# Streaming encoder step: attention scores from stacked high and low parts, two maps a step, layers written out

## What is computed

```python
for l in range(DEPTH):                       # DEPTH = 2
    h = rms_norm(x, norm_mix[l]);  q, k, v = split(h @ w_in[l])      # q and k normalised per head
    A: 6 heads of 64, window of 128, T5 bias, a learned sink:   p = exp(s-m) / (sum + exp(sink-m))
    B: 4 heads, two maps of 32 each, T5 bias:  p = softmax(s1) - lam * softmax(s2)
    C: 6 heads of 64, causal, s += cum_q - cum_k (forget gates)
    x = x + concat(A, B, C) @ w_out[l]
    x = x + (silu(h2 @ w_gate) * (h2 @ w_up)) @ w_down               # h2 = rms_norm(x, norm_ffn[l])
```

## Time and profile before

| | |
|---|---|
| median of 3 runs | 3513.45 us (3509.74 to 3520.22) |
| the profiled execution's span | 3514.1 us |
| TensorE busy | 3223.0 us (92%) |
| VectorE / ScalarE busy | 1718.7 us (49%) / 1076.7 us (31%) |
| mean granted TensorE clock | 0.967 of 2.4 GHz |
| DMA | 275 MB, 27.5% of 16 engines |
| first layer: project, attend, mix, feed | about 137 to 408, to 824, to 942, to 1797 us |
| second layer, same stages | about 1840 to 2120, to 2537, to 2655, to 3514 us |

### The profile page before, as it was taken

How to read it: one execution, slowest core, us unless ns; L and a number is a source line. 1 busy time by engine, 2 the same in 40 slices (tenths; PEclk the granted TensorE clock), 3 DMA queues, 4 the chain that set the end, 5 groups by cost and what they waited for, 6 DMA issues and landing times. The chain is left out here.

```text
span 3514.1 us, 50348 instructions
## 1 busy us (share of the span) xinstructions
PE 3223.0 (92%) x18146; PEld 2884.4 (82%) x18146; DVE 1718.7 (49%) x4094; ACT 1076.7 (31%) x2321; POOL 54.3 (2%) x32
## 2 busy tenths in 40 slices
PE   0699899998899999999969997999898999999999
PEld 0589777786789999999958896777777999999998
DVE  0444378643244544545445445785434454454454
ACT  1332276553221111111123225665423111111111
POOL 0000010000000000000000001010000000000000
PEclk9899999998999999999989998999998999999999
DMA  7244544333021111111024445525132111111111
GB/s 170 79 138 133 161 122 106 88 82 116 18 66 36 41 49 36 53 37 36 24 92 124 132 136 138 131 69 137 35 94 59 44 36 54 36 36 54 36 36 60
DMA packets 368396, 274.96 MB, mean 78 GB/s; under 512 B 128546, under 2 KB 336366, under 8 KB 368186
## 3 DMA queue, kind: packets, MB, share of 16 engines
q1 hardware_dynamic: 368218, 272.70, 27.5%
HBM read 195.84 MB, written 78.62 MB: 78 GB/s over the span
## 5 line engine op out<-in xcount | busy, mean ns | idle before, releaser
L1515 DVE TENSOR_TENSOR x<-x,ffn_down 128x512 f32<-128x512 f32 x792 | 509.4, 683 | 0.0
L1537 DVE TENSOR_TENSOR ffn_xn<-ffn_xn,ffn_up 128x384 f32<-128x384 f32 x132 | 73.1, 554 | 758.1 <-ACT ffn_xn L1482 758.1
L418 PE MATMUL ffn_up<-ffn_h_hi,ffn_hi_g 128*128 128x384 f32 x1056 | 360.3, 341 | 15.2 <-DVE ffn_h_lo L243 10.5
L419 PE MATMUL ffn_up<-ffn_h_lo,ffn_hi_g 128*128 128x384 f32 x1056 | 359.7, 341 | 0.0
L420 PE MATMUL ffn_up<-ffn_h_hi,ffn_lo_g 128*128 128x384 f32 x1056 | 359.4, 340 | 0.0
L418 PE MATMUL ffn_up<-ffn_h_hi,ffn_hi_u 128*128 128x384 f32 x1056 | 355.2, 336 | 3.2 <-DVE ffn_lo_u L243 3.2
L420 PE MATMUL ffn_up<-ffn_h_hi,ffn_lo_u 128*128 128x384 f32 x1056 | 354.8, 336 | 0.0
L419 PE MATMUL ffn_up<-ffn_h_lo,ffn_hi_u 128*128 128x384 f32 x1056 | 354.8, 336 | 0.0
L991 PE MATMUL att_S<-att_kT,att_qT 128*128 128x512 f32 (+3 forms) x864 | 322.9, 490 | 33.1 <-DMA att_qT<-scratch_qkT 25.9
L1482 ACT ACTIVATE ffn_xn<-ffn_up 128x384 f32<-128x384 f32 x132 | 64.9, 491 | 861.1 <-PE ffn_up L420 861.1
L418 PE MATMUL prj_acc<-prj_w_hi,prj_h_hi 128*128 128x384 f32 (+2 forms) x864 | 318.8, 369 | 0.0
(11 more groups left out here) (173 smaller groups left out, 5352.5 us busy)
## 6 DMA issues: line engine op xcount, KB each, us to landing
ffn_raw_g<-in_w_gate SPq DMA_DIRECT2D x44, 512.0 KB, 4.0
ffn_raw_u<-in_w_up SPq DMA_DIRECT2D x44, 512.0 KB, 5.1
ffn_raw_d<-in_w_down SPq DMA_DIRECT2D x44, 512.0 KB, 5.1
scratch_qkv<-prj_nat SPq DMA_DIRECT2D x72, 192.0 KB, 1.9
prj_w_raw<-in_w_in SPq DMA_DIRECT2D x64, 192.0 KB, 2.6
scratch_qkv<-prj_nat SPq DMA_DIRECT2D x36, 256.0 KB, 2.1
att_kT<-scratch_qkT SPq DMA_DIRECT2D x16, 576.0 KB
att_vn<-scratch_qkv SPq DMA_DIRECT2D x16, 576.0 KB, 8.4
```

Of the source, the lines that this page charges most:

```text
L418: pe.matmul(out, l_hi, r_hi, start=first, stop=False)
L419: pe.matmul(out, l_hi, r_lo, start=False, stop=False)
L1515: dve.tensor_tensor(x, x, down[:, (q * ND + n) % 4, :], ALU.add).then_inc(added, 1)
L1537: dve.tensor_tensor(a32[:, b, :], sg[:, b, :], up[:, b, 1, 0:384], ALU.mult).then_inc(gated, 1)
```

## The change

The two layers are written out instead of looped, and semaphores and tiles get the layer's number (`att0_scored`). Beyond that:

1. **project** splits the transposed q and k into high and low parts (`tT_hi` on ScalarE in place of the copy, `tT_lo` a new subtraction on VectorE, `cut_turned`) and stores both (`qk`), where it stored one. Sample rows are also stored whole (`qk_s`). The store of all rows to `scratch_qkv` shrinks to the value columns (`v`). `tT` has two buffers, not four.
2. **attend, scores**: in `qS` the 128 contraction rows hold the high part over the low part of one map's q; `kS` holds the key's high part twice (first matmul) and its low part twice (second). In B, with 32 rows a map, all four products fit one matmul. The data are f32r. Scores against cached keys stay float32.
3. **attend, steps**: a unit in A and C is now two heads (9 units a group), and in B one head with two maps (18) as before. Every unit has two jobs.
4. **attend, softmax**: the reduction forms bias minus score with its minimum, so its result is the exponential's bias and the one-column instructions go. The sink enters as column 0 of s. In C a column of ones behind v gives the row sum.
5. **attend, samples**: in A and C one matmul multiplies both heads; the result goes to `mixTb` without being turned back. A1 and A2 reuse A0's cached keys and values.
6. **memory**: x is given up during `attend`; `mix` reloads it (4 MB and 0.5 MB) behind the loads of g = 3. POOL no longer clears q.

```diff
@@ build
-        with nc.Fori(0, DEPTH) as layer:
+        for layer in range(DEPTH):
             project(nc, t, k, layer)
+            stream.close()
             attend(nc, t, k, layer)
+            stream = ExitStack()
+            k["x"] = stream.enter_context(nc.sbuf_tensor(f"x_{layer}", [P, T, D_MODEL], F32))
             mix(nc, t, k, layer)
             feed(nc, t, k, layer)
...
@@ project, VectorE
+            def cut_turned(u):
...
+                dve.wait_ge(taken_qk, m + 1)
+                split_lo(dve, tT_lo[:, m % 2, 0:n], turn[:, m % 2, 0:n], tT_hi[:, m % 2, 0:n]).then_inc(cut_qk, 1)
...
@@ attend, SP: load_front of A and C
-                for m in range(g.maps):
-                    sp.dma_start(qT[m * g.D:(m + 1) * g.D, b, m, :], t["qkT"][g.q_row(m):g.q_row(m) + g.D, :]).then_inc(sem, 16)
+                        sp.dma_start(qS[:, b, m, :].bitcast(F32), rows(t["qk"], q0, [[half, 2], [TOK, HEAD], [1, TOK]])).then_inc(sem, 16)
+                        if g.new_keys:
+                            for part in range(2):
+                                sp.dma_start(kS[:, b, 2 * m + part, :].bitcast(F32),
+                                             rows(t["qk"], part * half + k0, [[0, 2], [TOK, HEAD], [1, TOK]])).then_inc(sem, 16)
...
@@ attend, TensorE: score
+                    ks = [m] if g.kind == "B" else [2 * m, 2 * m + 1]
...
-                            last = pe.matmul(out[:, c:c + w], q, kT[:, b, k0 + c:k0 + c + w], start=True,
-                                             stop=not (g.kind == "C" and c + w == n))
+                            for x in ks:
+                                last = pe.matmul(out[:, c:c + w], q, kS[:, b, x, k0 + c:k0 + c + w], start=(x == ks[0]), stop=(x == ks[-1] and not masks))
...
@@ attend, VectorE: front
-                    dve.tensor_tensor_reduce(s[:, job % 2, 0:n], S[:, job % 2, 0:n], extra_row, 1.0, -3e38, ALU.add, ALU.max, mx[:, one]).then_inc(biased, 1)
+                    dve.tensor_tensor_reduce(s[:, r, g.sink:g.sink + n], S[:, r, 0:n], extra_row, -1.0, low, ALU.add, ALU.min,
+                                             bias[:, job:job + 1]).then_inc(biased, 1)
...
@@ mix, SP and VectorE
+                if g == 3:
+                    sp.dma_start(k["x"][:, 0:TP, :], t[prompt].rearrange("a (t p) d -> p (a t) d", p=P)).then_inc(x_in, 16)
+                    sp.dma_start(k["x"][:, TP, :], t[sample].rearrange("b s d -> (b s) d")).then_inc(x_in, 16)
...
+            dve.wait_ge(x_in, 32)
```

More of the change, by code:

```diff
@@ L123, in _ @@
                 numbers = sorted(s.num for s in self.sems)
-                assert numbers == list(range(numbers[0], numbers[-1] + 1))
-                pool.sem_clear(range(numbers[0], numbers[-1] + 1))
+                first = 0
+                for n in range(1, len(numbers) + 1):
+                    if n == len(numbers) or numbers[n] != numbers[n - 1] + 1:
+                        pool.sem_clear(range(numbers[first], numbers[n - 1] + 1))
+                        first = n
         self.ctx.close()
@@ L433, in stores @@
         flat = f"({shape})"
+        if name[2] == "v":
+            out.append((t["v"][i * P:(i + 1) * P, V_AT[first]:V_AT[first] + count], src))
         if sample:
@@ L494, in project, with samples_before @@
     order = [sum(bool(NORMED[v[0]]) for v in work[:u]) for u in range(NW)]
+    def samples_before(m):
+        return sum(work[normed_units[x]][1] == TP for x in range(m))
     def splits_at(u):
@@ L849, in attend @@
         for c in range(g.past_chunks):
-            extra.setdefault(g.index * UG + 2 + c, []).append(("past", g, c))
-        for c in range(3):
-            extra.setdefault((g.index + 1) * UG + 7 + c, []).append(("mix", g, c))
-    N_ITER = NU + 11
+            extra.setdefault(begin[g.index] + 2 + c, []).append(("past", g, c))
+        after = begin[g.index + 1] + (7 if g.kind == "B" else 3)
+        for c in range(3 if g.kind == "B" else 2):
+            extra.setdefault(after + c, []).append(("mix", g, c))
+    N_ITER = NU + 6
     order = []
@@ L952, in _ @@
                     load_front(groups[g.index + 2])
-                sp.wait_ge(evacuated, place["mix", g.index, 2] + 1)
+                sp.wait_ge(evacuated, last_mix[g.index])
+                if g.kind != "B":
+                    sp.wait_ge(taken_T, before(begin[g.index + 1], direct))
                 sp.dma_start(t["mixT"][g.tile * P:(g.tile + 1) * P, :], mixTb[:]).then_inc(mix_stored, 16)
@@ L999, in score @@
                                       start=(c == 0), stop=(c == g.nb - 1))
[L1000 removed]
+                        for x in ks:
+                            last = pe.matmul(out[:, g.n_past:g.n_samp], q, kS[:, b, x, SEQ:TOK], start=(x == ks[0]), stop=(x == ks[-1]))
                     last.then_inc(scored, 1)
@@ L1034, in turn_extra @@
                     elif c == 0:
-                        pe.wait_ge(taken_out, (g.index + 1) * UG)
+                        pe.wait_ge(taken_out, before(begin[g.index + 1], lambda *x: not direct(*x)))
                     a, e = chunk_of_mix(c)
@@ L1262, in mix @@
 def mix(nc, t, k, layer):
-    ph = Phase(nc, "mix")
+    ph = Phase(nc, f"mix{layer}")
     BANKS = 8
```

442 lines of the change are left out of this document (258 added, 184 removed).

## The result

The changed kernel takes **4254.8 us** (median of 4 runs, 4253.3 to 4264.9) against 3514.0 for the kernel before: a ratio of **1.212**, 95% interval 1.210 to 1.214. It is 741 us slower. I had forecast 3419 with a range up to 3465, so the prediction was wrong in sign and by 836 us.

A forecast was written before the change was run, and what follows sets the result against it. TensorE was taken to bound project and attend, with VectorE close behind in B and taking over there. Per layer A -12, B -25, C -19, end -2, mix +10.5 make -47.5, twice -95: 3419 us, range 3380 to 3465.

The forecast's parts named there:

- Loads, start of attend: Attend: extra q and k bytes at 340 to 390 GB/s cost A0 +6.5 us, B0's front +1, later groups nothing.
- loads weigh more: Rival, loads of q and k: at 250 GB/s about 13 us a layer more, 3445 us; chance 0.13.
- The slow case: Rival, B: TensorE's clock stays at half level throughout, 3557 us, slower than before; chance 0.02.
- A: Attend's A groups: cheaper scores and no turning back save 3.2, 4.1 and 4.1 us; POOL's dropped clearing of qT saves 8.
- B: Attend's B groups: VectorE becomes the limit, 111 us instead of 139.2, -28, and +3 for B0's cached keys.
- hand-overs: B: pauses between engines add 3 us to the limiting engine's work.
- My signs for B: Profile after, B: 111 to 115 us, VectorE busy over 90%, TensorE near 80%; a clock below 0.9 would be wrong.
- C: Attend's C groups: TensorE stays the limit; -5.6 us a group and -2 for POOL's clearing in C0, -19 a layer.
- The rival of the narrow pieces: Rival, scores of 128 or 256 columns: they cost what float32 costs, 3495 us; chance 0.03.
- Mix: Mix: reloading x delays g = 4's loads, a stall of 8 us and +2.5 for the half-level clock, together +10.5.
- Project: Project: 26 us more VectorE work is hidden, 0; if the cover fails in the first nine units, +4.
- The milder one: Rival, B: TensorE's clock falls for half of its 90 us, +8 to +12 a layer, 3437 us; chance 0.10.

The follow-up runs named there:

- e1: Changed kernel with the first two dimensions of the source pattern exchanged in every load of qS and kS, row number outermost: 3446.1 us.
- e4: e1 with each of B's loads of qS and kS writing every second one of all 128 partitions in place of 64 neighbouring ones: 3422.1 us.
- e5: e4 with mix's load of x put behind the loads of g = 7 in place of g = 3: 3418.2 us.
- e8: The kernel of e4 again, in more rounds and on the same chip as e9: 3427.3 us.
- e9: The kernel of e5 again, in more rounds: 3417.8 us.
- e10: e9 with project's subtraction that forms the low part of q and k run on 1 column in place of 256 to 512: 3415.4 us.

## Why the prediction was wrong, step by step

**Loads, start of attend: the step that failed.** It counted bytes (3.5 MB for A0, 6.1 for B0) and divided them by the rate of the earlier trace rows. But that rate is one of transfers with 32 to 128 rows outermost, and the change replaces these by transfers with a pair outermost. The diff in the section on the change shows it, `[[half, 2], [TOK, HEAD], [1, TOK]]`, and I read past it. What I put down as +6.5 for A0's loads was, in TensorE's waits, 77.7 us in place of 13.1: +65. B0's front, +1, was 78.0. A1's loads, which I took as nothing, cost 57.1, and those of B1 and C, "in the shadow", 66.4 and 131.4. What failed is the rate, and with it the overlap. My rival "loads weigh more" had the right place, but its worst rate was 250 GB/s, four times what the trace of after shows (63), so even the range left the real cause out. The slow case that I did name, a clock that stays down through B, is not what made the kernel slower: with the loads mended the same work takes 3446.1. A rate taken from a trace belongs to the shape of transfer that made it.

With this one term mended (e1), the rest of the sum can be held against what happened. Layer 1, from the ends of groups and stages in e1's trace and in that of before (attend starts with POOL's first clearing, 411.8 us before and 416.1 in e1):

| part | forecast, us | measured in e1, us |
|---|---|---|
| start of attend to A2's end (B0's wait left out) | -13 | 95.4 to 75.5: -20 |
| B with B0's waits | -24 | 139.2 to 135.8: -3 |
| C and the end of attend | -21 | 195.9 to 177.2: -19 |
| mix | +10.5 | 99.5 to 104.0: +4.5 |
| project | 0 | +4 (and +8 in layer 2; see below) |
| loop written out | 0 | 11.7 to 7.3 between the layers: -4, once |
| both layers and the whole | -95 | 3514.1 to 3447.6: -66.5 |

**A: right mechanism, too small.** A2 takes as long as A1 once POOL no longer clears qT, as forecast. The group ends of e1 show both at 19.5 us (forecast: 22):

```profile
452.67 0.95 POOL L1035 MEMSET att_qpast<- 128x1024 f32 x1 [35.54 <-PE att_S L1070]
472.15 0.95 POOL L1035 MEMSET att_qpast<- 128x1024 f32 x1 [18.53 <-PE att_S L1070]
491.62 0.95 POOL L1035 MEMSET att_qpast<- 128x1024 f32 x1 [18.52 <-PE att_S L1070]
```

In A1 TensorE is busy for all of it, 19.50 of 19.50 us; before it was 25.18 of 26. The saving of 6.5 is 5.7 of work and 0.8 of pauses; I had counted 4.1. By the distances between starts the scores fell from 7.9 to 4.4 us (-3.5, where I had -2.7), the rest of the work by 2.2 (where I had 1.4): the samples' matmuls, which I had not counted, are part of it. The remaining clearings of qpast cost nothing that shows.

```profile
453.60:473.10 19.50, 19.50 (x174) 19.45 (x174) 11.79 (x57) 15.18 (x51) 0.97 (x2) 1.00 0.37 123
```

**B: the waits and TensorE's work were too small.** Of the 21 us that e1's B fell short, e4 gives back 8 (B takes 128.0 there) through the packets' length. The rest went where I had 3 us of hand-overs. My signs for B failed too: VectorE was to be busy for over 90% of it and is for 74% in e1 and 78% in e4. TensorE's work is 105.0 us in e1 and not 90, as much as VectorE's. Of the 15 us more, about 9 are an estimate for the half clock (18.6 us of the work ran at it). The other 6 are not split further; part of them is the first score matmul of a map, behind which the next one starts after 0.31 us and not 0.23. A sum of each engine's work over a group assumes that the slower one works without pause, and 569 to 593 us show that the two take turns: 61.6 us in B1 where VectorE's work alone is 54. VectorE's work itself, 100 us in B0 and B1, was less than my 107.5.

**C: right.** TensorE stays the limit (forecast 49.4 us a group; C1 takes 51.7). The prices held. TensorE in e1's C1, where a unit of 1024 keys has two heads:

```profile
709.00 1.17 PE L1061 MATMUL att_S<-att_kS,att_qS 128*128 128x512 f32 x4
710.00 0.23 PE L1063 MATMUL att_S<-att_mask_b,att_ident_b 128*128 128x128 bf16 x1
710.04 1.17 PE L1061 MATMUL att_S<-att_kS,att_qS 128*128 128x512 f32 x4
711.06 0.23 PE L1063 MATMUL att_S<-att_mask_b,att_ident_b 128*128 128x128 bf16 x1
```

Two pieces of 512 columns in two passes take 1.0 us, start to start, where before the same took 1.78. Behind the first matmul of a head the next starts after 0.31, 0.26, 0.20 and 0.14 us for 512, 384, 256 and 128 columns; behind the others after 0.23, 0.17 and 0.12, the three values that I used, and 0.06 for 128. For a piece of 128 columns in two passes that makes 0.20, near my 0.22. The rival of the narrow pieces falls.

**Mix: right mechanism, too large.** The pause before g = 4 is 3 us instead of 8, because x came at 400 GB/s and TensorE reached g = 4 a us later than before; and no fall of the clock followed, for which I had 2.5. (The 8 were themselves a slip: 14 us of x behind 857.76 make 872 and not 870, a pause of 10.)

**Project: a little more than nothing.** It takes 4 us more in layer 1 of e1 and 8 in layer 2, but the 8 is one profile: in the changed kernel, e4, e5, e8 and e9 the second layer has 1.6 to 4.5 more than before, the first 3.3 to 5.5. e10 gives some 1 to 3 us of this to the subtraction; where the rest and the shorter step between the layers (-4) come from, no run tells.

**The clock.** In e1's B it is 0.84 and 0.94 on average, 0.89 over both groups and 0.85 in layer 2: below the 0.9 that I had named as a sign against me. In B0 the two low levels begin within the waits for transfers (12.0 and 4.5 us); in B1 there is one, for 6.8 us from 587.9, after pauses of 0.5 and 2.3 us. It did not stay down through B, so the rival of the slow case falls. The milder one came true in part: 18.6 us of TensorE's work in layer 1 and 28.4 in layer 2 ran at the half level, where I had thought of 45, and that is 9 and 14 us of TensorE time. How much of this made B longer, and so what e1 would gain at the full level throughout, was not tried.

**What the 95 would have been.** e9's 3417.8 us is 1.2 us from the forecast of 3419. That is no merit of the sum: e9 has three edits that I did not foresee, and terms that were off in both directions cancel (A and mix came out lower than forecast, B and project higher). It is luck.

## What to carry to other kernels

When a transfer's access pattern changes, ask what its outermost dimension is before its bytes are divided by a rate: two entries outermost meant two packets in flight here, 69.6 us instead of 10.7 for the same 3.5 MB, and the remedy was to exchange two dimensions. Then look at the destination: transfers that all write 64 neighbouring partitions moved 220 GB/s where those over all 128 moved 397, with the engines busy in both. Two engines that trade the limit within a stage make it longer than either one's work; take the sum by stretches, not by stage.

## What was new about the hardware

- Packets in flight in these kernels: 2 with 2 entries outermost, 4 with 4, about 16 with 32 or 64, and no more when several such transfers stand in the queue. One packet of 4608 bytes took 178 ns (median) in all these cases.
- The same packet took 352 ns when each transfer wrote 64 neighbouring partitions, and 178 again when these were every second one of 128.
- Behind an f32r matmul of 128 columns the next starts after 0.06 us, half of a float32 instruction of that width (0.11); behind the first of a head or map it is 0.14.
